# Stick breaking attention moved into the projections' stage, with the last two convolutions' products between its transposes and scores

## What is computed

```
proj = xn @ w_comb
c_b, c_c, c_x = jnp.split(proj[..., :OFF_SB], 3, axis=-1)
y_conv = c_b * causal_dwconv(c_c * c_x, conv_w)          # 512 channels, 3 taps
q, k, v = jnp.split(proj[..., OFF_SB:OFF_GATE], 3, axis=-1)
y_sb = stick_breaking_attention(to_heads(q), to_heads(k), to_heads(v))   # 8 heads of 64
y_rwkv, v_first = rwkv7_time_mix(proj[..., OFF_RWKV:], ...)
```

## Time and profile before

| | |
|---|---|
| median of 3 runs | 2080.5 us (2079.74 to 2082.56) |
| the profiled execution | 2083.53 us, its span 2081.8 us |
| PE busy | 97% of the span |
| DVE, ACT, POOL busy | 51%, 38%, 6% |
| mean granted TensorE clock | 0.978 of full speed |

### The profile page before, as it was taken

One profiled execution on the slowest core, in us unless ns is written; L12 is line 12 of the kernel. 1 busy time (PEld: TensorE's weight loads), 2 busy tenths in 40 slices (PEclk: granted clock), 3 DMA queues, 4 the chain that ended last, 5 costly groups with the idle time before them and its releaser, 6 DMA issues. The chain is left out here.

```text
span 2081.8 us, 29325 instructions
## 1 busy us (share of the span) xinstructions
PE 2010.3 (97%) x11736; PEld 1616.2 (78%) x11736; DVE 1067.3 (51%) x1763; ACT 795.3 (38%) x1273; POOL 135.0 (6%) x173
## 2 busy tenths in 40 slices
PE   8999879999999999999999999998999999999997
PEld 6678647868888877788888777886777788888886
DVE  5666375455445634567776234227655554423433
ACT  5432352243323533444443213325666544322421
POOL 0000136500000000000000001000001000000000
PEclk9999979999999999999999999999999999999998
DMA  4233200013232331222223414222111222223232
GB/s 178 67 126 117 86 1 23 3 53 111 91 102 93 122 132 41 81 87 95 101 91 116 161 68 129 92 91 74 46 45 42 78 95 91 98 94 102 91 101 81
DMA packets 48593, 181.95 MB, mean 87 GB/s; under 512 B 5504, under 2 KB 5888, under 8 KB 47840
## 3 DMA queue, kind: packets, MB, share of 16 engines
q1 hardware_dynamic: 44240, 165.61, 23.5%
q0 software_dynamic: 3088, 12.90, 1.8%
q10 hardware_dynamic: 1152, 1.89, 0.3%
HBM read 175.08 MB, written 5.29 MB: 87 GB/s over the span
## 5 line engine op out<-in xcount | busy, mean ns | idle before, releaser
L209 DVE TENSOR_TENSOR weights_lo<-weights_raw,weights_hi 128x1024 fp32r<-128x1024 f32 (+2 forms) x288 | 364.4, 1265 | 800.1 <-ACT weights_hi L201 799.6
L201 ACT ACTIVATE weights_hi<-weights_raw 128x1024 fp32r<-128x1024 f32 (+2 forms) x288 | 313.5, 1088 | 838.2 <-PE sp_ps L234 251.2
L232 PE MATMUL sp_ps<-arena_parts,weights_hi 128*128 128x512 f32 x720 | 284.2, 395 | 3.0 <-DVE arena_parts L303 2.5
L233 PE MATMUL sp_ps<-arena_parts,weights_hi 128*128 128x512 f32 x720 | 282.0, 392 | 0.0
L234 PE MATMUL sp_ps<-arena_parts,weights_lo 128*128 128x512 f32 x720 | 282.0, 392 | 0.0
L232 PE MATMUL end_ps<-arena_parts,weights_hi 128*128 128x512 f32 x576 | 225.1, 391 | 0.5 <-DVE arena_parts L305 0.5
L234 PE MATMUL end_ps<-arena_parts,weights_lo 128*128 128x512 f32 x576 | 224.5, 390 | 0.0
L233 PE MATMUL end_ps<-arena_parts,weights_hi 128*128 128x512 f32 x576 | 224.4, 390 | 0.0
L232 PE MATMUL fr_ps<-arena_parts,weights_hi 128*128 128x512 f32 (+1 forms) x480 | 182.6, 380 | 2.1 <-DVE arena_parts L305 1.1
L233 PE MATMUL fr_ps<-arena_parts,weights_hi 128*128 128x512 f32 (+1 forms) x480 | 180.8, 377 | 0.0
L234 PE MATMUL fr_ps<-arena_parts,weights_lo 128*128 128x512 f32 (+1 forms) x480 | 180.8, 377 | 0.0
(11 more groups left out here) (389 smaller groups left out, 3002.8 us busy)
## 6 DMA issues: line engine op xcount, KB each, us to landing
weights_raw<-w_up SPq DMA_DIRECT2D x44, 512.0 KB, 3.5
weights_raw<-w_proj SPq DMA_DIRECT2D x38, 512.0 KB, 3.5
weights_raw<-w_gates SPq DMA_DIRECT2D x32, 576.0 KB, 3.7
weights_raw<-w_ca SPq DMA_DIRECT2D x32, 512.0 KB, 3.4
weights_raw<-w_down SPq DMA_DIRECT2D x16, 704.0 KB, 4.1
weights_raw<-w_in SPq DMA_DIRECT2D x22, 512.0 KB, 3.5
weights_raw<-w_logits SPq DMA_DIRECT2D x16, 512.0 KB, 3.5
weights_raw<-w_ff1a SPq DMA_DIRECT2D x16, 512.0 KB, 3.4
```

Source lines behind the costliest of these rows:

```text
L201: act.activation(self.w_hi[:, g % 2, 0:cols], self.raw[:, g % 2, 0:cols], ACT.Copy).then_inc(self.hi_ready, 1)
L209: dve.tensor_tensor(self.w_lo[:, g % 2, 0:cols], self.raw[:, g % 2, 0:cols], self.w_hi[:, g % 2, 0:cols].bitcast(F32), ALU.subtract).then_ ...
L232: pe.matmul(out, left[0], right[0], start=start, stop=False)
L233: pe.matmul(out, left[0], right[1], start=False, stop=False)
```

## The change

Two stages become one. `proj_stage` runs its groups in another order: the time mix's 14, the six groups of convolutions 0 and 1, key, query (both now in other tiles, key in `core.h`), the four of the values, and last the six groups of convolutions 2 and 3. The time mix's turns come earlier and closer. The units of the attention start inside the value groups. Each of the last six groups is cut into two halves of four blocks (a **piece**, 12 in all), and a piece stands after the transposes of a unit and before the scores three units on. The convolutions are no longer stored and read back; instead `core.h`, used as scratch, is read again from the input in the next stage (2 MB instead of 1 MB).

More of the change, by code:

```diff
@@ L358, in h_split, with pe_by_token @@
     return Split(core, name, lambda k: core.h[:, k, :], parts or (lambda k: core.pair(XN_HI, XN_LO, k)), lambda k: core.v(gain, k))
-def pe_by_token(core, pe, groups, width, rhs, tiles, bank):
+def pe_by_token(core, pe, groups, width, rhs, tiles, bank, after=None):
     per = core.cols[core.used] // width
@@ L376, in pe_by_token @@
         core.used += 1
+        if after is not None:
+            after(q)
 class Spill:
@@ L617, in scaled_keys, with __init__, work, convolve @@
         dve.tensor_tensor(rate, rate, self.sums[:, c, :], ALU.mult).then_inc(self.b_made, 1)
+TURNS = {22: (0, 1), 23: (2, 3), 25: (4, 5, 6), 26: (7, 8, 9), 27: (10, 11)}
+class ConvLace:
+    FIRST, COUNT = 32, 6
+    BANKS = (6, 7, 6, 6, 7, 6)
+    def __init__(self, core, breaks):
+        self.core, self.breaks, self.g0 = core, breaks, core.used + self.FIRST
+        self.done, self.taken = core.sem("cl_done"), core.sem("cl_taken")
+        self.steps, self.convolved = core.sem("cl_steps"), core.sem("cl_convolved")
+        self.count = 0
+    def work(self, j):
+        return self.core.arena[:, 54, :], self.core.arena[:, 71, :], self.core.arena[:, j, :]
+    def piece(self, pe, p):
[20 more added lines that the diff above has]
+        dve.wait_ge(self.core.groups_done, self.g0 + t + 1)
+        if t == 3:
+            dve.wait_ge(self.convolved, 3)
+        dve.tensor_tensor(self.work(2 + t // 3)[t % 3], self.ps[:, self.BANKS[t], :], scale_at, ALU.mult).then_inc(self.taken, 1)
+    def convolve(self, dve, j, u, y, b):
+        core = self.core
+        def chained(ins):
+            self.count += 1
+            ins.then_inc(self.steps, 1)
+            dve.wait_ge(self.steps, self.count)
+        if j >= 2:
+            dve.wait_ge(self.taken, 3 * (j - 1))
+        chained(dve.tensor_tensor(u, u, y, ALU.mult))
+        chained(dve.tensor_scalar(y, u, core.v("conv_w", 8 + j), None, ALU.mult))
+        chained(dve.scalar_tensor_tensor(y[:, 1:T], u[:, 0:T - 1], core.v("conv_w", 4 + j), y[:, 1:T], ALU.mult, ALU.add))
+        chained(dve.scalar_tensor_tensor(y[:, 2:T], u[:, 0:T - 2], core.v("conv_w", j), y[:, 2:T], ALU.mult, ALU.add))
+        dve.tensor_tensor(core.arena[:, j, :], y, b, ALU.mult).then_inc(self.convolved, 1)
@@ L639, in proj_stage @@
     rest_ready, shared, conv_ready = core.sem("proj_rest_ready"), core.sem("proj_shared"), core.sem("proj_conv_ready")
-    first_cols = 2 * P
+    first = slice(3 * P, 5 * P)
+    breaks = StickBreaking(core)
+    lace = ConvLace(core, breaks)
+    breaks.lace_taken = lace.taken
     conv = lambda j, i: core.arena[:, 26 + 3 * (j % 2) + i, :]
     with ExitStack() as ctx:
-        ps = ctx.enter_context(nc.psum_tensor("proj_ps", [P, 4, T], F32))
-        ps_v = ctx.enter_context(nc.psum_tensor("proj_ps_v", [P, NT, T], F32))
+        whole = ctx.enter_context(nc.psum_tensor("proj_ps", [P, 8, T], F32))
+        ps, ps_v = whole[:, 0:4, :], whole[:, 4:8, :]
+        breaks.ps = lace.ps = whole
         scale = TokenScale(core, "mix_in", [core.arena[:, 40 + n, :] for n in range(2)], ps_v[:, 0, :], scale_at,
@@ L671, in _ @@
                     tm.gpsimd_gate(pool, c)
-                tm.gpsimd_bonus(pool, 0)
                 for c in range(NW):
[L674 to L678, removed]
+                    tm.gpsimd_bonus(pool, c)
                 pool.wait_ge(tm.bonuses.out, 16 * NW)
                 pool.wait_ge(tm.gates.out, 16 * NW)
+                pool.wait_ge(tm.b_made, NW)
+                pool.wait_ge(lace.convolved, 2)
+                pool.wait_ge(const_in, 32)
+                breaks.constants(pool)
+                for u in range(breaks.units):
+                    breaks.mask(pool, u)
             @block.tensor
@@ L738, in _ @@
                 act.wait_ge(rest_ready, 2)
-                for n in range(2, 38):
+                for n in range(2, 28):
                     core.split_hi(act, g0 + n + 2)
@@ L795, in blend @@
                     dve.scalar_tensor_tensor(q[:, 1:T], p[:, 0:T - 1], core.v("mu_rwkv", o), q[:, 1:T], ALU.mult, ALU.add).then_inc(mixed, 1)
[L797 to L812, removed]
                 def add(k):
@@ L857, in _ @@
                 scale.invert(dve)
-                for n in range(38):
+                for n in range(28):
                     if n == 0:
@@ L865, in _ @@
                         core.split_lo(dve, g0 + n + 2)
-                    if n < 34:
-                        take(n)
+                    take(n)
                     if 1 <= n < 15:
@@ new lines, in _, with later @@
+                    if n in (17, 20):
+                        j = (n - 17) // 3
+                        dve.wait_ge(core.banks_free, 4 + e0 + 14 + 3 * j + 3)
+                        if j == 0:
+                            dve.wait_ge(tm.gates.out, 16 * NW)
+                        lace.convolve(dve, j, conv(j, 0), conv(j, 1), conv(j, 2))
+                def later(n):
+                    core.split_lo(dve, g0 + n)
+                later(30)
+                breaks.weigh(dve, 0)
+                later(31)
@@ new lines, in _ @@
+                breaks.weigh(dve, 1)
[9 more added lines that the diff above has]
+                lace.take(dve, 1, scale_at)
+                later(35)
+                breaks.weigh(dve, 6)
+                breaks.weigh(dve, 7)
@@ new lines, in _ @@
+                lace.take(dve, 2, scale_at)
+                later(36)
+                breaks.weigh(dve, 8)
[10 more added lines that the diff above has]
+                lace.take(dve, 5, scale_at)
@@ L3404, in _constants @@
     c["neg_tri"][:] = -1.0 * (row >= col)
-    c["neg_ones"][:] = -1.0
-    c["neg_diag_t"][:] = np.where(row < col, 0.0, NEG)
-    for n in range(7):
+    for n in range(6):
         b = 1 << n
```

288 lines of the change are left out of this document (126 added, 162 removed).

## The result

The changed kernel takes 2062.97 us in the median of 5 runs (2062.2 to 2069.8); the kernel before takes 2080.07 us in the runs beside it (2078.84 to 2082.56). The ratio is 0.9921, 95% interval 0.9907 to 0.9934: 17.1 us or 0.8% faster. Of the five runs, four lie between 2062.2 and 2063.63 us at a mean granted clock of 0.985 or 0.986; the fifth took 2069.8 us at 0.934. On another chip the changed kernel has a median of 2063.47 us (6 runs) and the kernel before, beside it, one of 2082.56 (11 runs, 2077.41 to 2087.02): 19.1 us by the medians, 16.9 by the ratio of 0.9919. The forecast was 2060.0 (2054.5 to 2072). The profiled execution took 2062.97 us, its span 2061.1.

The account below looks back on a forecast made before the run. PE, busy for 97% of the span, was taken as the bound. The new stretch of 72.0 us saves 25.5 of 97.5, less 5.0 for clock: 20.5 us, so 2063.0 on the profile's terms, 2060.0 as median (2054.5 to 2072).

Parts of the forecast that it names:

- The walk of the four lists: From group 24 to the end, four engines' lists laid side by side: PE waits 1.0 us at unit 2's transposes.
- At the turns: Time mix's turns 8 and 11 and the places ahead of the values: 4.6 us of new PE waits together.
- unit 2's: PE's wait at the transposes of unit 2, behind value copies, two places and four sigmoids on ACT: 1.0 us.
- the tail's: End of the merged stage: PE idles 4.6 us while DVE finishes the last convolution and takes the output.
- Two charges of 2.5 us: Half clock in the first value group and at the chunks stage's start: 2.5 us taken for each.
- 61.8 us: PE's work for the six moved groups (32.6) and the attention's pairs (29.2), at full clock without waits.
- the old stretch: Last value product to next stage's first product, before the change: 29.2 work + 20.85 idle + 14.9 half clock = 64.9 us.
- The stalled ring: Rival, chance 0.10: units wait for ACT as now, 11.5 us; gain only 9 us, 2071.5 us.
- the 0.5 us to spare: ACT's slack between scores of u + 3 and u + 4, after sigmoids and a placing: 0.5 us.
- The swinging clock: Rival, chance 0.06: the clock keeps falling and rising in the merged stretch, 21 us longer, 2076.0 us.
- Half clock throughout: Rival, chance 0.04: the merged work is held at 1.2 GHz, about 60 us lost against 25.5 won, 2115 us.
- The last rival: Chance 0.03: pieces don't fill the gaps; waits and half clock stay, only the work's place changes, 2080 us.

Follow-up runs that it names:

- the second profile: The kernel before, unchanged, run and profiled again: 2080.78 us, ratio 1.0002; its profiled execution has a span of 2076.7 us.
- the laced kernel: The changed kernel itself, with pieces standing between the steps of the attention's units, against the kernel before: 2062.97 us, ratio 0.9921.
- the one that isn't laced: The changed kernel with its six groups straight behind the value groups, ahead of all transposes, nothing between units: 2081.78 us, ratio 1.0002 to the kernel before.
- three reorderings together: The changed kernel with turns placed before splits, convolution 3 started earlier, and unit 2's scans and products before group 33's low part: 2053.48 us.

## Why the prediction was right, and where it was off

**What bounds.** Right: PE alone. The walk of the four lists named the four waits that remain and no other above 0.2 us; the trace has the same four.

**The waits.** At the turns 1.45, 1.45 and 1.7 us were forecast, 1.25, 1.25 and 1.29 measured; unit 2's 1.0, measured 1.29; the tail's 4.6, measured 4.70. The causes are shown by the edits that remove them.

**The clock.** Two charges of 2.5 us were forecast. The half clock came at both places: 3.4 us long in the first value group (1.7 us of cost), 6.8 us long at the chunks stage's start. There the stage takes 129.4 us from its first product to the front region's, where it took 127.8: 1.6 us. Both lie in the bounds; 5.0 was taken, 3.3 it was. Full clock inside the stretch came as forecast, but the reason given, that the old stage has it where its waits are short, isn't what the rows show: from 271.6 to 281.8 us the old stage held 1.00 with PE busy for 6.37 of 10.20 us and waits of 0.74 and 2.12 us.

```profile
199.60:203.00 3.40, 3.40 (x10) 2.62 (x9) 0.00 (x0) 0.00 (x0) 0.00 (x0) 0.51 0.18 75
...
291.80:298.60 6.80, 6.38 (x26) 3.64 (x28) 4.00 (x8) 0.00 (x0) 2.86 (x4) 0.50 0.79 304
```

**The work.** 61.8 us was too little. The stretch 168.60 to 292.20 is 123.6 us; less eight groups (43.5) and eight turns (3.6) it leaves 76.5, where the forecast has 72.0 and a charge of 2.5. Waits (9.8) and half clock (1.7) leave 65.0 us of work, 3.2 more than forecast. A pair takes 15.90 us and not 7.30 + 8.16 = 15.46, with no idle time in it: a piece between transposes and scores costs 0.15 us more than its 12 matmuls in a row. That accounts for 1.8 of the 3.2 us. Whole groups right behind transposes show the same, 5.58 us (180.77 to 186.35) in place of 5.44, which is part of the rest; I can't place all of it.

**The base.** On the terms of the profiled execution the forecast was 2063.0, and the profiled execution took 2062.97. That it fits so well is luck. The span is 20.7 us shorter where 20.5 was forecast: the work was 3.2 us more, the waits 0.4 and the half clock 1.7 less, and the rest of the kernel, of which the forecast said nothing, 1.3 less. As a median the forecast was 2060.0, and 3.0 us off. The term that was mis-sized is the old stretch: it was taken from one profile of the kernel before, 3.0 us above the median, and the gain was then taken from the median. In the second profile the old stage is 3.75 us shorter (5.3 us less for half clock, 1.5 us more idle time). With that the gain would be 20.5 - 3.75 = 16.8 us and the median forecast 2063.7; the measured gains of 17.1 and 19.1 us lie between 16.8 and 20.5.

**Slips in the working.** By the prediction's own charges (3.4 and 10 us) its upper bound is 2068.4 and not 2066, still inside the range. The tail's steps add up to 6.9 us, 4.6 less PE's 2.3 and not 4.3; DVE ended 4.4 us behind PE. PE's longest single wait of the kernel before, 8.9 us for low parts of weights, lies outside the stick breaking stage; the largest sum lies in it. And the half clock of 20.5 us began at 251.1 us, inside the idle time of 3.87 us and not behind it.

**The rivals.** The stalled ring didn't come: a pair has no idle time. But with whole groups it did (6.6 us of placing), so the 0.5 us to spare was no slack to count on, and the halves are what kept it. The swinging clock didn't come in the laced kernel (1.00 in both pairs) and did in the one that isn't laced (0.81), where waits of 1 to 2 us stand. The passage of the Trainium skill that the prediction set beside this rival ("TensorE: Matmul & The Clock Gate", section "A second HAM failure mode: psum-queue depth-cycling") names both the cycling through PSUM banks and the short idle times between groups of matmuls. Banks are cycled in both kernels here, so the cycling alone doesn't bring it; the idle time differs, and so does the mix of products between the waits, which these runs don't separate. Half clock throughout didn't come. The last rival, that nothing would be filled, has its own kernel in the one that isn't laced: 1.0002.

**The transfer.** The read of 2 MB lands 7.8 us after its issue at the start of a stage of 129 us. Nothing waited for it.

## What to carry to other kernels

Where a chain over several engines leaves the matrix engine short waits of 1 to 2 us, work without any tie to the chain was worth most when it was cut into pieces a little longer than the wait (2.72 us) and put behind each step that causes one; the same work in one block ahead of the chain brought nothing here, and in pieces of twice the size 7.1 us, where the halves brought 17 to 19. Before trusting the gain, look at what the interleaving leaves at both ends: small steps that queue behind a split, and the last convolution after the last product, cost 8.5 us of PE's waiting and 3.3 of half clock, and three reorderings together won 10 us of that and of its surroundings. And take the base of a forecast from more than one profile if a stage is partly at half clock.

## What was not expected of the hardware

A stretch of half clock doesn't need one long wait. In the changed kernel the longest wait of PE ahead of it is 1.29 us; the last two, 2.5 us in all, stand 0.66 us apart, and 3.4 us of half clock follow. With one wait of 0.74 us there is none. Idle time doesn't always bring it, either: the old stage held full clock from 271.6 to 281.8 us with PE busy for 62% of the time, and was held at 0.50 from 251.1 to 271.6 us with PE busy for 66%. And it can come without any idle time: in the kernel before, PE is busy without a gap from 80.0 to 97.4 us, yet from 90.6 us on the clock is at 0.50 for 6.8 us. From 87.63 us on, ahead of the fall, PE makes eight products of only 8 rows (8x512, 4.24 us in all). Whether they are the cause is not shown by these runs. Last, the same kernel can lose 14.9 or 9.6 us to half clock in the same stage with nearly the same waits (20.9 and 22.4 us in all), which is more than many changes bring.
